# Split activations moved by 32 bytes against the weight slots, within each 128 bytes

## What is computed

```
x = x + merged @ w_out
x = x + peer_ffn(rmsnorm(x), w_query, keys1, keys2, expert_u, expert_v)     # 16384 experts, gate G per token
for layer in range(2):
    x = x + 0.5 * ((silu(h @ w_gate) * (h @ w_up)) @ w_down)                # h = rmsnorm(x); D_FF = 2816
    x = x + mixer(rmsnorm(x))                                               # stick-breaking, then block attention
    x = x + 0.5 * swiglu(rmsnorm(x), ...)
```

## Time and profile before

| | us |
|---|---|
| median of 3 runs | 2041.19 |
| lowest and highest run | 2041.07, 2041.62 |
| span of the profiled execution (first to last instruction) | 2039.6 |
| PE busy, share of the span | 2005.6, 98% |
| DVE busy, share | 1508.3, 74% |
| ACT busy, share | 1123.1, 55% |

### The profile page before, as it was taken

How to read it: one execution, slowest core, us unless ns; L and a number is a source line. 1 busy time by engine, 2 the same in 40 slices (tenths; PEclk the granted TensorE clock), 3 DMA queues, 4 the chain that set the end, 5 groups by cost and what they waited for, 6 DMA issues and landing times.

```text
span 2039.6 us, 37233 instructions
## 1 busy us (share of the span) xinstructions
PE 2005.6 (98%) x13232; PEld 1822.9 (89%) x13232; DVE 1508.3 (74%) x2564; ACT 1123.1 (55%) x1835; POOL 59.9 (3%) x40
## 2 busy tenths in 40 slices
PE   7999999999999999999999999999999999999998
PEld 6999999988888888888888999999999999999998
DVE  5868898877777777777777667776667667957666
ACT  5445537965555555555555555755555555655554
POOL 0000430000000000000000000000000000000000
PEclk9999999999999999999999999999999999999999
DMA  6445543055565666655665555455555555445553
GB/s 214 135 135 190 205 142 104 24 174 187 189 192 192 187 189 192 191 189 187 206 231 173 187 186 174 135 169 188 187 186 178 185 185 186 156 143 177 185 188 111
DMA packets 101466, 353.73 MB, mean 173 GB/s; under 512 B 11392, under 2 KB 16640, under 8 KB 101120
## 3 DMA queue, kind: packets, MB, share of 16 engines
q1 hardware_dynamic: 100944, 350.13, 52.5%
q10 hardware_dynamic: 432, 2.36, 0.3%
HBM read 348.77 MB, written 3.67 MB: 173 GB/s over the span
## 4 chain that ended last, share of the span: by engine, by line
PE 90%; DVE 7%; ACT 2%; issue 1%; DMA 0%; SPq 0%; DVEq 0%; ACTq 0%
PE front L2030 38%; PE acc L2030 35%; PE tile L2030 16%; DVE w_lo L1219 2%; ACT w_hi L715 1%; DVE rstd L1241 1%; ACT h_parts L741 0%; DMA raw<-stream 0%; PE front L2587 0%; DVE cand L1688 0%; DVE h_parts L1248 0%; DVE sq L1230 0%; DVE conv L1573 0%; DVE rest L1657 0%; DVE top_i L1653 0%
## 5 line engine op out<-in xcount | busy, mean ns | idle before, releaser
L1219 DVE TENSOR_TENSOR w_lo<-raw,w_hi 128x1024 fp32r<-128x1024 f32 x612 | 747.0, 1223 | 85.4 <-ACT w_hi L715 84.9
L715 ACT CAST w_hi<-raw 128x1024 fp32r<-128x1024 f32 x628 | 654.3, 1044 | 137.6 <-PE tile L2030 60.8
L2030 PE MATMUL front<-h_parts,w_hi 128*128 128x512 f32 (+1 forms) x2432 | 586.4, 377 | 4.2 <-ACT h_parts L741 2.5
L2030 PEld LDWEIGHTS front<-h_parts,w_hi 128*128 128x128 f32 x2432 | 436.5, 189 | 80.2 <-issue 2.4
L2030 PE MATMUL front<-h_parts,w_lo 128*128 128x256 f32 x2272 | 337.2, 282 | 0.0
L2030 PEld LDWEIGHTS front<-h_parts,w_lo 128*128 128x128 f32 x2272 | 318.8, 190 | 20.6
L2030 PE MATMUL tile<-h_parts,w_hi 128*128 128x256 f32 x1344 | 247.8, 286 | 5.1 <-DVE w_lo L1219 2.6
L2030 PEld LDWEIGHTS tile<-h_parts,w_hi 128*128 128x128 f32 x1344 | 209.5, 192 | 8.2 <-issue 4.9
L1304 DVE TENSOR_TENSOR scaled<-front,scaled 128x512 f32<-128x512 f32 x76 | 52.6, 692 | 215.1 <-ACT scaled L779 215.1
L2030 PE MATMUL acc<-w_hi,mid_hi 128*128 128x512 f32 x512 | 200.9, 392 | 2.1 <-DVE mid_lo L1793 1.7
L783 ACT ACTIVATE scaled<-scaled 128x256 f32<-128x256 f32 x188 | 78.6, 418 | 223.4 <-DVE scaled L1307 116.6
(11 more groups left out here) (324 smaller groups left out, 2519.5 us busy)
## 6 DMA issues: line engine op xcount, KB each, us to landing
raw<-stream SPq DMA_DIRECT2D x632, 512.0 KB, 3.7
early_u<-stream SPq DMA_DIRECT2D x20, 512.0 KB, 3.6
early_activations<-early_out SPq DMA_DIRECT2D x20, 128.0 KB, 3.5
scaled<-early_activations SPq DMA_DIRECT2D x10, 128.0 KB, 4.0
x<-x_t SPq DMA_DIRECT2D x2, 512.0 KB, 5.3
keysT<-keys_t ACTq DMA_DIRECT2D x1, 1024.0 KB, 6.3
attc<-attention_constants ACTq DMA_DIRECT2D x1, 1024.0 KB, 7.1
out_t<-h SPq DMA_DIRECT2D x4, 256.0 KB, 2.4
```

Source lines behind the costliest of these rows:

```text
L715: nc.scalar.copy(w_hi[:, s, :], raw[:, s, :]).then_inc(hi_ready, 1)
L1219: nc.vector.tensor_tensor(w_lo[:, s, :], raw[:, s, :], w_hi[:, s, :].bitcast(F32), ALU.subtract).then_inc(lo_ready, 1)
L2030: return nc.tensor.matmul(out, lhsT, rhs, start=start, stop=stop, **kw)
```

## The change

A constant `SHIFT` of 8 words (32 bytes) is added to `H_HI`, and `H_LO` and `MID` follow. `COLS` is moved up by 8 + 24 = 32 words (128 bytes) in all, and everything behind it too, so those tiles keep their place within 128 bytes.

```diff
-H_HI = 3 * RING * D
+SHIFT = 8
+H_HI = 3 * RING * D + SHIFT
 H_LO = H_HI + KT * T
 MID = H_LO + KT * T
-COLS = MID + 5 * 2 * T
+COLS = MID + 5 * 2 * T + 32 - SHIFT
 ONES = COLS + P
```

## The result

The changed kernel takes 2043.94 us in the median (2042.02 to 2046.33 over 20 runs), the kernel before, run beside it, 2041.18 us (2040.64 to 2042.13, also 20). The ratio is 1.0014 with a 95% interval from 1.0007 to 1.002: 2.8 us slower, real, but inside the 0.2% that the prediction counted as no change. The 2016 us that it forecast are 28 us away. The traced span is 2041.7 us, 2.1 more than that of before.

The account below looks back on a forecast made before the run. PE was taken to bound the kernel, with 90% of the chain. Gains of 11.6, 5.0 and 10.2 us sum to 26.8; 95% of it, 25.4, off 2041.2 gives 2016 us, range 1985 to 2050.

Parts of the forecast that it names:

- What bounds the kernel: Whole kernel: PE bounds, busy 2005.6 of 2039.6 us and holding 90% of the chain, at the 2.4 GHz level.
- The mechanism: Float32r matmuls: reads of both operands hinder each other, PE settles in multiples of 32 cycles, 13.3 ns extra each.
- Nothing changes: Rival for all matmuls: PE settles again in the same step whatever the start, 2041 us; chance 0.16.
- The narrow terms: 256-column matmuls of drains, projections and feeds: 11.6 us and 5.0 us won.
- 4128 x 2.8: 256-column matmuls at 120.0 ns, in feed-forward drains and projections: 2.8 ns less each, 11.6 us won.
- 2272 by 2.2 ns: 256-column matmuls behind a wide run: from 119.4 to 117.2 ns each, 5.0 us won.
- The `y` stretches: Branch projections (117.8 ns) and end of the w_o projections (116.7), already in the new relation: mean 117.2 ns, should stay.
- the term of the wide matmuls: 512-column matmuls in feeds and PEER drains: 2.8 ns less on each of 3648, 10.2 us won.
- the wide matmuls lose their step: Rival for 512-column matmuls: they stay at 235 ns, 21.9 us lost, 2046 to 2063 us; chance 0.22.
- the early scores: Plain float32 matmuls with 256 columns, 215.9 ns each, whose spacing should stay.
- 95% of a gain: From PE's gain to the kernel's end: 95% of 26.8 us gets through, 25.4 us.

Follow-up runs that it names:

- both_moved: All tiles, weights too, moved 32 bytes further against the kernel before: 2041.44 us, ratio 1.0001.
- the row of matmuls: Separate kernel of float32r matmuls alone, each of 64 pairs of streamed and loaded places: at equal places 120.0 ns at 256 columns, 226.7 at 512.
- h64_peer0: Against the kernel before, h, y and the feed-forwards' mid tiles 64 bytes above the weights, the PEER loop's mid level with them: 2025.30 us, ratio 0.9920.
- shift64: The change with 64 bytes in place of 32 for h and mid, against the kernel before: 2033.25 us, ratio 0.9956.

## Why the prediction was wrong

**What bounds the kernel** held. PE stays at 98% and the granted clock, but for the 3.4 us near the start, at 1.00, and the change came by spacings and the waits behind them.

**The mechanism** held in its main point: the step depends on the distance of the two operands. `both_moved` (nothing changes) and the row of matmuls (moved by one letter, the same durations) show that it is the distance and not a place; that it is the two reads which hinder each other is my reading, and no run took the load away. The finer part, steps in multiples of 32 cycles, didn't hold: at the 2.4 GHz level 116.7 ns are 280 cycles, 113.3 are 272 and 233.3 are 560. *Nothing changes* was the rival in mechanism: every group of spacings moved, so it fell, although its time, 2041, came nearer than mine. "SBUF — State Buffer", section "SBUF: two separate sides", of the Trainium skill has PE waiting for nobody at the memory; here the same float32r instruction goes from 113.3 to 120.0 ns by addresses alone, and the measurement decides. The formula of "TensorE: Matmul & The Clock Gate", section "Back-to-back issue gap", of the Trainium skill, N/2.4 + 2.5 ns for an isolated step, holds here for bfloat16 (109.15 and 215.85 ns, where it gives 109.2 and 215.8), and not for float32r.

**The narrow terms** were about right: "4128 x 2.8" and 2272 by 2.2 ns, 16.6 us in all; measured 18.8, with 3.33 ns for each matmul of the drains and 2.44 for those with `h` streamed. The `y` stretches, the same relation on this side of the change, were a fair sample for this width (117.4 ns where PE doesn't wait, against the 117.2 taken). Two slips of the sum are small: 160 of the 2272 stand behind no wide run, and 416 more narrow matmuls with `h` streamed, which the sum leaves out, gain too.

**The failed step** is the term of the wide matmuls: "I take 2.8 ns, by the nearest row, because the settled extra is the same 13.3 ns at both widths: 3648 x 2.8 = 10.2 us". Measured: 4.5 ns more on each feed and 4.7 on each PEER drain, 16.7 us lost, 26.9 us away from the term. The same extra at one place says nothing about how it moves: in the row of matmuls the narrow step falls from 120.0 to 116.7 ns between 0 and 32 bytes while the wide one rises from 226.7 to 233.3, and 226.7 is the lowest of all places. The rival *the wide matmuls lose their step* came true, and at its own deciding point of 4.6 ns; it had reckoned with 6. Its reason for doubt, that PEER drains have the opposite distance, proved no difference: 32 and 224 bytes cost the same at 512 columns (233.3 and 233.4). The forecast missed by this one term. That the result stands near 2041, the time of *nothing changes*, is a coincidence: two opposite changes of 18.8 and 16.7 us.

**y was not untouched.** I wrote that "the y stretches and the early scores should stay". The tiles behind `COLS` moved by 32 floats, 128 bytes, which is no move modulo 128 but half a period modulo 256: `y` went from a difference of 32 to one of 160 and from 117.4 to 118.3 ns, 0.5 us. My period came from the 512 bytes between successive blocks, which can't tell 128 from 256.

**What passes to the end.** I let 95% of a gain through. The spacings give 1.6 us, and the end came 2.1 us later, so 3.7 us stand in waits, in the projections and around the norms. With 18.8 us won on the narrow matmuls this is a fifth, not a twentieth, though the 0.6 us of `both_moved` show that some of it comes without any new spacing.

**The sum again, with measured terms:** -18.8 + 16.7 + 0.5 + 3.7 = +2.1 us, the difference of the two spans (2041.7 and 2039.6). The medians differ by 2.8; the rest stands in the spread, which also grew (1.5 us over 20 runs before, 4.3 after).

## What to carry to other kernels

The time of a float32r matmul from start to start depends on where its streamed operand lies relative to the loaded one, with another best place for each width and each neighbour: take no term for one width from a sample of another. Before placing tiles, run the kernel's own sequence of matmuls alone with the places as the variable (it agreed with the kernel to 0.001 us in every PEER step and in most feed-forward steps, but it showed only one of the two steps that a stage at 64 bytes can settle in), then choose a place for each stage by its mix of widths. Here that brought 0.7%, no more than `h64_peer0` (0.8%), whose places came from the table of single widths. When tiles are shifted, pad what lies behind them to a full 256 bytes, so that nothing else moves with them.

## What the runs showed of the hardware

- **The period is 256 bytes, in steps of 16 at least.** At 256 columns the step lies between 113.3 and 120.0 ns, at 512 between 226.7 and 236.7. The best places differ: 64 and 112 bytes for the narrow, 0 for the wide.
- **Only float32r does it.** Plain float32 (111.67 ns at 128 columns, 215.84 at 256, for each of the two rows that a matmul has in the trace) and bfloat16 (109.15 at 256, 215.85 at 512) have the same step at the four places tried.
- **It is not a count of loaded columns.** With 64 loaded columns in place of 128 the steps at 0, 32, 64 and 96 bytes were 113.3, 117.8, 113.3 and 118.3 ns at 256 streamed columns, and 229.7, 230.7, 228.4 and 230.0 at 512. At 512 columns the extra over 213.3 ns didn't halve (16.4 ns at 0 bytes, where 128 loaded columns have 13.4), at 256 it did at 0 bytes and didn't elsewhere, and the order of the places changed.
- **Two settled steps at one place.** At 64 bytes a row of 256-column matmuls ran at 113.3 ns, and at 117.8 behind a series of 192 columns; in the kernel whole stages hold one or the other. With this comes a wider spread of run times (2026.33 to 2036.84 in `shift64`, where the kernel before stays within 1.5 us). A stage in the slow one is 2.0 us longer (178.65 against 176.62 us in `shift64`), so four of them could make up 8 of those 10 us; that is an estimate, since only one execution of each kernel was traced.
- **Fewer than 256 columns saved next to nothing, and the clock fell there.** Steps of 64 columns took 111.7 ns at the 2.4 GHz level, hardly less than 256 columns do; four times the granted clock fell to the 1.2 GHz level in such a series or just behind it, and there 64, 128 and 192 columns all took 213.3 ns.

What stays open is the mechanism inside: I know that the distance of the two operands decides, and not the absolute place, and that the settled steps need no traffic of other engines; the number of loaded columns changes the values, but not in proportion. Which banks or lines are fought over, and why another width turns the order of the places around, no run here shows, and neither what chooses between two settled steps at the start of a stage.
